# Another order of transfers between routing and last stage, and the low parts of five U blocks on VectorE

## What is computed

```python
s = jnp.einsum('chpk,hpnk->chpn', q, sub_keys).astype(jnp.float32)
top_s, top_i = lax.top_k(s, K)                       # 16 best of 128 keys, both halves
cand = top_s[:, :, 0, :, None] + top_s[:, :, 1, None, :]
best_s, best_j = lax.top_k(cand.reshape(C, PEER_HEADS, K * K), K)
...
e = i1 * N_KEYS + i2                                 # expert number
g = jax.nn.softmax(best_s, axis=-1).astype(x.dtype)
u = jnp.take(expert_u, e, axis=0)
h = jax.nn.gelu(jnp.einsum('cd,chkd->chk', x, u))
v = jnp.take(expert_v, e, axis=0)
return jnp.einsum('chk,chkd->cd', g * h, v)
```

## Time and profile before

| | |
|---|---|
| median of 3 runs | 3397.34 us (3393.84 to 3401.84) |
| profiled execution | 3392.29 us, its span 3390.5 us |
| TensorE (PE) busy | 3220.7 us, 95% |
| VectorE (DVE) busy | 2525.0 us, 74% |
| ScalarE (ACT) busy | 1316.4 us, 39% |
| GpSimd (POOL) busy | 1114.5 us, 33% |
| bytes moved by DMA | 774.22 MB, 228 GB/s over the span |

### The profile page before, as it was taken

The page is one execution under the profiler, slowest core; times in us unless marked ns, Lnnn a source line. Parts: engine busy times, 40 slices in busy tenths (PEclk is TensorE's granted clock), DMA queues, the critical chain, the costliest instruction groups (busy, mean ns, idle before and its releaser), DMA issues.

```text
span 3390.5 us, 53956 instructions
## 1 busy us (share of the span) xinstructions
PE 3220.7 (95%) x17714; PEld 2838.4 (84%) x17714; DVE 2525.0 (74%) x4172; ACT 1316.4 (39%) x2269; POOL 1114.5 (33%) x631
## 2 busy tenths in 40 slices
PE   7999999899889999999999999998998899999999
PEld 6787799888878888888877877998988788888877
DVE  3555499999578888888645554999984888888876
ACT  4343323344343443343334433223443433444433
POOL 4343344200234343332044434542002333433410
PEclk9999999999999999999999999999999999999999
DMA  3211244577789999989622113445777899999995
GB/s 120 69 50 56 100 132 134 171 294 285 284 304 347 348 321 335 339 321 336 224 101 69 49 56 103 137 133 193 281 291 286 305 329 341 344 343 339 332 331 204
DMA packets 242561, 774.22 MB, mean 228 GB/s; under 512 B 19536, under 2 KB 124112, under 8 KB 207312
## 3 DMA queue, kind: packets, MB, share of 16 engines
q1 hardware_dynamic: 205520, 503.53, 42.7%
q0 software_dynamic: 36864, 268.45, 21.5%
HBM read 689.59 MB, written 82.31 MB: 228 GB/s over the span
## 4 chain that ended last, share of the span: by engine, by line
DVE 30%; PE 28%; issue 14%; DMA 12%; DVEq 10%; ACT 3%; POOL 1%; ACTq 0%; SPq 0%; POOLq 0%
PE PS L448 8%; PE PS L450 8%; PE PS L449 8%; DVEq L1448 7%; DMA VRAW<-in_peer_v 6%; DMA RAW<-in_peer_u 4%; DVE ROWS L1366 4%; DVE VLO L1434 4%; DVE X L1372 3%; DVE OB L1400 2%; ACT VHI L1001 2%; DVEq L1399 2%; PE PS L615 2%; DVE EQS L1321 1%; POOL RL L1475 1%
## 5 line engine op out<-in xcount | busy, mean ns | idle before, releaser
L448 PE MATMUL PS<-XH,RH 128*128 128x384 f32 (+1 forms) x2720 | 983.0, 361 | 21.5 <-POOL RL L1475 15.9
L1475 POOL TENSOR_TENSOR RL<-RAW,RH 128x1024 fp32r<-128x1024 f32 x304 | 756.2, 2497 | 748.2 <-ACT RH L800 747.5
L450 PE MATMUL PS<-XH,RL 128*128 128x384 f32 (+1 forms) x2720 | 955.6, 351 | 0.0
L449 PE MATMUL PS<-XL,RH 128*128 128x384 f32 (+1 forms) x2720 | 953.5, 351 | 0.0
L1509 POOL DMA_INDIRECT ROWS<-in_peer_rows,LIST x256 | 290.2, 1134 | 1359.4 <-DVE X L1372 1314.0
L448 PE MATMUL PS<-VHI,WHI 128*128 128x512 f32 x1536 | 605.4, 394 | 40.0 <-DVE WLO L1437 40.0
L449 PE MATMUL PS<-VLO,WHI 128*128 128x512 f32 x1536 | 603.8, 393 | 0.0
L450 PE MATMUL PS<-VHI,WLO 128*128 128x512 f32 x1536 | 603.7, 393 | 0.0
L448 PEld LDWEIGHTS PS<-XH,RH 128*128 128x128 f32 x2720 | 514.5, 189 | 49.4 <-POOL RL L1475 16.5
L449 PEld LDWEIGHTS PS<-XL,RH 128*128 128x128 f32 x2720 | 515.0, 189 | 27.1
L450 PEld LDWEIGHTS PS<-XH,RL 128*128 128x128 f32 x2720 | 513.1, 189 | 28.6
(11 more groups left out here) (230 smaller groups left out, 3418.1 us busy)
## 6 DMA issues: line engine op xcount, KB each, us to landing
RAW<-in_peer_u SPq DMA_DIRECT2D x256, 512.0 KB, 3.8
VRAW<-in_peer_v SPq DMA_DIRECT2D x256, 512.0 KB, 5.8
RAW<-in_stream SPq DMA_DIRECT2D x128, 512.0 KB, 3.2
route_dram<-STAGE SPq DMA_DIRECT2D x16, 3072.0 KB, 11.8
GC<-route_dram SPq DMA_DIRECT2D x64, 768.0 KB, 10.3
gelu_dram<-GS SPq DMA_DIRECT2D x152, 192.0 KB, 3.6
GB<-gelu_dram SPq DMA_DIRECT2D x32, 768.0 KB, 12.1
GEL<-gelu_dram SPq DMA_DIRECT2D x6, 768.0 KB, 7.4
```

The lines of the kernel that those rows point to most:

```text
L448: pe.matmul(acc, sh, mh, start=first, stop=False)
L449: pe.matmul(acc, sh, ml, start=False, stop=False)
L450: return pe.matmul(acc, sl, mh, start=False, stop=last)
L1475: pool.tensor_tensor(RL[:, k % 4, :], RAW[:, k % 2, :], RH[:, k % 4, :].bitcast(F32), ALU.subtract).then_inc(S.low_part, 1)
```

## The change

On SP, between the last routing store and U80, the order becomes: U76, U77, wait for the first gelu stores, GB, GS72, wait for the stores of both STAGE buffers, GC first half, U78, V0, V1, GS73, U79, GC second half, GS74, GS75, U80, U81. The low parts of U73 and U74 go to VectorE, ahead of the two row additions that stand behind the routing, and those of U75, U76 and U77 to VectorE behind them. GpSimd keeps the two gathers, waits until the low parts up to U77 are counted, and makes those of U78 to U81 as before.

```diff
--- before.py
+++ after.py
@@ -395,28 +395,37 @@
                                 load_hidden(it + 2, 0)
                                 load_hidden(it + 2, 1)
 
-                sp.wait_ge(S.routing_stored0, count(l, "routing_stored0", 64))
-                apart(sp)
+                def load_next(n):
+                    load_experts(J_U + FILLED + n, FILLED + n, n % 2)
+
+                def load_gelus_of_first():
+                    for s in range(4):
+                        sp.wait_ge(sems[f"gelu_stored{s}"], count(l, f"gelu_stored{s}", 16))
+                        apart(sp)
+                    sp.dma_start(GB[:], gelus.rearrange("(g i) p t -> p g i t", i=QUAD)[:, 0]).then_inc(S.gelu_loaded, 16)
+
+                def routing_kept():
+                    for s in range(2):
+                        sp.wait_ge(sems[f"routing_stored{s}"], count(l, f"routing_stored{s}", 64))
+                        apart(sp)
+
+                def load_routing_of_first():
+                    sp.dma_start(GC[:, 0].rearrange("p b i t -> p b (i t)"),
+                                 route.rearrange("b p (g i) t -> p g b (i t)", i=QUAD)[:, 0]).then_inc(S.routing_loaded0, 16)
+
+                load_next(0)
+                load_next(1)
+                load_gelus_of_first()
+                store_gelu(FILLED - 4, 0)
+                routing_kept()
+                load_routing_of_first()
+                load_next(2)
                 position(0, 0)
                 position(0, 1)
-
-                def load_next(n):
-                    load_experts(J_U + FILLED + n, FILLED + n, n % 2)
-
-                load_next(0)
-                load_next(1)
-                store_gelu(FILLED - 4, 0)
-                load_next(2)
                 store_gelu(FILLED - 3, 1)
-                sp.wait_ge(S.routing_stored1, count(l, "routing_stored1", 64))
-                apart(sp)
-                for s in range(4):
-                    sp.wait_ge(sems[f"gelu_stored{s}"], count(l, f"gelu_stored{s}", 16))
-                    apart(sp)
-                load_filled(0)
-                store_gelu(FILLED - 2, 2)
                 load_next(3)
                 load_new(0)
+                store_gelu(FILLED - 2, 2)
                 store_gelu(FILLED - 1, 3)
                 load_next(4)
                 load_next(5)
@@ -1410,9 +1419,13 @@
                             dot((k + 1) % RING, (k + 1) // RING)
 
                 for k in range(S_ROUTE, S_ROUTE + S_TURN):
+                    low(0, J_U + FIRST + R_FILLS + 1 + k - S_ROUTE)
                     add_row(k, k % RING)
                     dot((k + 1) % RING, (k + 1) // RING)
                     dve.drain()
+                for n in range(J_U + FIRST + R_FILLS + 1 + S_TURN, J_U + FILLED + 2):
+                    low(0, n)
+                dve.drain()
 
                 def position(it, q):
                     n = 8 * it + q
@@ -1522,12 +1535,11 @@
                 for i in range(8):
                     for k in range(2):
                         gather(2 * i + k + RING)
-                pool.wait_ge(S.low_part, count(l, "low_part", J_U + FIRST + R_FILLS + 1))
-                n = J_U + FIRST + R_FILLS + 1
                 for k in range(S_TURN):
-                    low_of(n + k)
                     gather(S_ROUTE + k + RING)
-                for n in range(n + S_TURN, J_U + FILLED + 6):
+                pool.wait_ge(S.low_part, count(l, "low_part", J_U + FILLED + 2))
+                apart(pool)
+                for n in range(J_U + FILLED + 2, J_U + FILLED + 6):
                     low_of(n)
                 for it in range(16):
                     for q in range(8):
```

## The result

The changed kernel takes 3379.64 us (median of 7 runs, 3375.76 to 3388.29) against 3395.09 for the kernel before, measured again beside it: ratio 0.995, 95% interval 0.9934 to 0.9965, so 15.5 us faster where 13.5 were forecast. Two later comparisons gave less: 9.6 us (ratio 0.9975, 0.9957 to 0.9993) and 8.7 us (0.9983, 0.9965 to 1.0). The three average 11.2 us, and the interval of the last reaches no change at all, so that the first came out so near the forecast is in part luck. The profiled execution took 3375.76 us, its span 3374.0.

A forecast was written before the change was run, and what follows sets the result against it. TensorE, busy 95%, was bound with holes between routing and last stage, set by U79's chain. Gains of 6.8 + 6.7 = 13.5 us take 3392.29 to 3378.8; with 5.05 for the median, 3383.8 us, range 3374 to 3395.

The forecast's parts named there:

- The place and the chain: Passage from routing to last stage: U79's landing, then U81, then V0's low part, set the first pair, at 946.5.
- The terms of the sum: Earlier first output pair in each layer: 6.8 us in layer 0 and 6.7 in layer 1, together 13.5 us.
- The exclusion between GpSimd and VectorE: V0's low part on VectorE cannot run beside GpSimd's low part of U81; 1.1 us a layer either way.
- the 16.8 us from U79 to the pair: Kernel before, layer 0: from U79's landing to the first output pair, called 16.8 us of fixed order.
- The order on SP: SP's new queue behind the routing store: U76 lands 916.1, U77 919.2, GC 924.2, U79 929.5.
- U76 takes V0's place: In the queue behind the routing store U76 lands when V0 did, 916.1, leaving a first TensorE hole of 2.1 us.
- The clock: TensorE after its first hole in the passage: hole near 2 us, without low clock after it.
- the gap before the third block: TensorE's idle time before its third U block in the passage, to be about 4.5 us.
- The low parts on VectorE: Low parts of U73 to U77, 1.23 us each on VectorE: cost nothing; without cover 6.2 us a layer.
- Rival (c): Last stage loses the shift through more waits for V loads, 3409 to 3435 us if slower; chance 0.15, 0.08 slower.
- The sign that I gave for it: Rival (c) holds if the stretch behind the first pair is longer by more than 3 us a layer.
- The bad end of the range: GC and GB cost about 7 us each from issue to landing as today, leaving 2 us gain a layer.

The follow-up runs named there:

- The four kernels above: Kernels with low parts of U73 to U77 on VectorE, differing only in V0/V1 and GC/GB order on SP; passages 46.0 (changed kernel) to 50.1 us in layer 0 where listed.

## Why the prediction came out right

**The place and the chain: right.** The forecast put U79 at 929.5 and the pair at 946.5; they came at 930.7 and 947.28. GC landed at 924.5 for 924.2, U81 at 937.46 for 936.4. The terms of the sum were 6.8 and 6.7 us a layer and measured 6.1 and 6.4. In layer 0 the missing 0.7 us is U79, 1.1 us later after the store than forecast (29.4 for 28.3), less 0.4 by which the rest of the chain was shorter (16.6 for 17.0).

The exclusion between GpSimd and VectorE was there (2.60 us), and taking it away gave 1.2 us together with the other low parts. Its price was entered too low: 2.59 - 1.23 is 1.4 us a layer, not 1.1, which is only the time by which VectorE's instruction outlasts GpSimd's. Nor are the 16.8 us from U79 to the pair fixed, as the text has it: with U79 moved ahead of V0 they grew to 19.5 (928.16 to 947.63), since U81 did not come earlier with it.

**The order on SP: right for the whole, off for U76.** "U76 takes V0's place" was to land it at 916.1; it came at 917.4, and the hole was 3.22 us instead of 2.1. Most of that is not the order: the routing store ahead of U76 took 12.7 us to land instead of 11.8, so it was in at 914.0 and not at 913.0, and behind it U76 is another 0.3 us late. It did not matter, since U77 came at 919.6 for 919.2 and the chain begins there. The run with V0 and V1 ahead of U76 shows the same more sharply.

**Which part gains: not separated.** The forecast costs the new order as a whole. The four kernels above give most of it to GC and GB (3.4 to 4.7 us a layer) and the lesser part to V0 and V1 (0.3 to 1.6).

**The clock: wrong in layer 0, right in layer 1.** I expected no low clock after the first, shorter hole. In layer 0 the window from 920 to 925 was granted 0.50 of full speed, the 1.2 GHz level, after a hole of 3.22 us; before the change the same window had 0.67. In layer 1, behind a hole of 2.71 us, the window from 2600 to 2605 was granted 1.00. The low clock costs TensorE some 2.5 us: U76 and U77 take 11.1 us (919.75 to 930.86) in layer 0 and 8.6 in layer 1. It also settles the gap before the third block, forecast at 4.5 us: 1.39 in layer 0, where the slow blocks fill it, and 4.30 in layer 1. In the end it costs nothing, as the pair waits for VectorE.

**The low parts on VectorE: priced at nothing lost; they gain nothing either.** The text gave the new chain VectorE's earlier low parts (918.5, 921.6) and found both before the turns of U78 and U79. It did not draw the conclusion that this half of the change could be dropped. The run with the order alone says so.

**What lies behind the pair: right here, but not safe.** The shift reached the end as far as the scatter lets one see: the passages give 12.5 us, and the three comparisons of times 15.5, 9.6 and 8.7. Rival (c), that the last stage gives the shift back, doesn't show in this kernel. The sign that I gave for it, 3 us more in a layer's last stage, is finer than the scatter: the third profile of the changed kernel has 755.7 us in layer 1 against 749.8 before, its first 747.1. A loss of 18.5 us did come as soon as the pair was pulled in front of U81. Its main cause was not the phase of gathers against loads that I had named, but a low part made late, that of U81: U83's load waited for it with V2 behind it on SP, and when V2 was put ahead, VectorE's dot products and the gathers behind the same low part held the pair up instead.

**The scatter.** I took TensorE's waits of 13.9 and 7.5 us as a property of the layers. They are not: in the twelve profiles whose last stage is unedited they run from 2.5 to 14 us.

**The bad end of the range: not worked out.** The text lets U79 land at about 934.5, 2 us gained, if GC and GB cost 7 us each. Put one after the other into its own list, 7 us each instead of 2.2 and 2.3 would land U79 at 939, later than before the change. What happened lies at the other end: GC landed 0.3 us from its forecast, 10.5 us after an early issue.

## What to carry to other kernels

When an engine issues all transfers in order, look for the load that waits on a computed result and ask what stands behind it that needs no such wait: put that in front, so that the queue works while the issuer waits. Find the one chain that decides the next stage and count the bytes ahead of its first transfer; a hole elsewhere in the busiest engine may cost little or nothing, as the hole of 7 us did here. But moving the first transfer of the chain moves the end only if its later links can follow, and U81 could not. And when work is pulled earlier, look at what its new order makes late, and who is queued behind that.

## What the runs showed of the hardware

TensorE's granted clock was 0.50 in the row from 920 to 925, behind a hole of 3.22 us; in the rows from 905 to 915 TensorE had been busy without a break at 1.00. In layer 1 the clock stayed at 1.00 behind a hole of 2.71 us (2600 to 2605). VectorE's two-input instructions beside GpSimd's low part lasted 2.6 us (V0's low part) and 3.4 us (a dot product) instead of 1.2, each time until about a microsecond after GpSimd's end. And the execution time of one kernel scattered by 25 us (3372.62 to 3397.07 for the changed one). Its three profiled executions (3375.76, 3376.09 and 3388.9 us) have the same passages within 0.2 us, and last stages that sum to 1485.8, 1489.8 and 1498.2 us, with 16.1, 19.1 and 25.2 us of TensorE's waits in them. Over the twelve profiles whose last stage is unedited, that stage takes 730 to 744 us in layer 0 and 741 to 759 in layer 1. That the V blocks land at varying times there is the likely source, not tried by itself.
